# GpSimd's low parts of the weights: one 1024-column instruction per unit in place of four of 256 columns

## The chip, the cores and the metric

The kernel runs on one core of a Trainium2 chip. A core has TensorE (PE in the profile), VectorE (DVE), ScalarE (ACT), GpSimd (POOL), and SyncE (SP), which here only issues transfers. They run side by side, each through its own list of instructions in order, and wait for one another with semaphores. Data lies in SBUF (128 partitions); products land in PSUM, whose tiles the profile calls `bank`. The metric is the device time of one execution in microseconds (us), lower being better; for the kernel before, the median of three runs.

## The reference

Two transformer blocks in float32, on x of 512 tokens by 1024 channels:

```python
def first_block(x, ...):
    h = rmsnorm(x, ln1[l])
    z = jnp.einsum('btd,de->bte', h, w_in[l])
    u_pool, gq, gk, gv, gg, ga, fq, fk, fv, ff = jnp.split(z, pts, axis=-1)
    y_pool = pool_mixer(u_pool, ...)       # trailing means over 2, 4, 8, 16 tokens
    y_gla = gla_mixer(gq, gk, gv, gg, ga, ...)   # gated linear attention, chunks of 64
    y_fox = fox_mixer(fq, fk, fv, ff, b_f[l])    # softmax attention with a forget term F
    x = x + jnp.einsum('btd,de->bte', concatenate([y_pool, y_gla, y_fox]), w_o[l])
    h = rmsnorm(x, ln2[l])
    gate, up = split(h @ w_gu[l])
    x = x + (silu(gate) * up) @ w_down[l]
    return rmsnorm(x, ln_f)

def second_block(x, ...):
    q_lat, c_kv, k_rope, z_a, q_b, k_b, v_b, z_b, q_idx, k_idx, w_idx, gate_a, gate_b = split(rmsnorm_2(x) @ w_in)
    y_a = mla_attention(...) * silu(z_a)   # 8 heads, keys and values out of a latent
    y_b = dsa_attention(...) * silu(z_b)   # top-128 keys of each query by an index score
    merged = sigmoid(gate_a) * (y_a @ w_o_a) + sigmoid(gate_b) * (y_b @ w_o_b)
    return rmsnorm_2(x + merged @ w_out)
```

All the weight matrices together are read once, as 162 pieces of 512 KB.

## The kernel before

Every float32 product is made of three products of rounded (fp32r) numbers: high part by high part, low by high, high by low (lines 1379, 1381 and 1383, or 1393 to 1395 and 1405 to 1407 where the weights are what moves or the width differs). So each weight is needed as a high and a low part.

**The stream of weights.** A unit is eight weight tiles of 128x128, a piece of 128x1024 float32. SP loads units in order into the three buffers of `WS` (line 1256). For unit u, ACT copies `WS` to `WH`, which rounds it (line 1565, 161 times); then DVE or GpSimd subtracts, `WL = WS - WH` (DVE at line 1816, GpSimd at line 2164); then PE may use the unit. `WH` and `WL` have four buffers. Which engine makes `WL` is decided when the unit's step is planned, by a Python variable: `now["low"]` is `w_low_v` (DVE) at first, `w_low_g` (GpSimd) from line 762, in the middle of the GLA stage, to the end of FoX and of `w_o` (line 811), DVE again for the feed-forward part, GpSimd from line 1047 through the attention of the second block, and DVE from line 1193. That makes 97 units for DVE and 64 for GpSimd.

GpSimd does a unit in four instructions of 256 columns. Each first waits for the GpSimd instruction before it (`before[0]`) and for the unit's high part. The first three report an intermediate name `(u, c)` for which no other engine waits; the last one reports u. For that report PE waits before the unit's first product, and SP before it loads unit u+3, since the `WS` buffer is read until then:

```python
def split_low(u):
    return unit_low[u](u)
...
    if n >= NST:                                   # SP, in load(); NST is 3
        q.wait_ge(split_low(n - NST))
    e.dma_start(WS[:, n % NST, :], wall[n])
```

**The order of the work.** A planner written in Python makes one list, `steps`; every engine's program goes through that list and picks its own instructions. Nothing is reordered later. So an instruction that waits holds up all that stands behind it on its engine.

GpSimd's other work: the trailing means (`p_a`, `p_d`, lines 2184 to 2197), the fills of the FoX stacks `f_s` and `f_m` (lines 2170 to 2176, four memsets for each of four stacks, the last four at about 133 us), sums of squares (`acc`, lines 2204 and 2207), the product of gate and up in the feed-forward part (`fa`, line 2212) and a merge (line 2216).

SP's other work matters at one place. A FoX stack takes its forget rows and a copy of its other half by transfers (`stack_rows`, lines 1288 and 1290, and `stack_high`, lines 1297 and 1301), and these stand in the same list of SP behind loads of units. PE's first logits of that pair (line 1480) wait for the transfer of `f_m`.

DVE's work beside its own low parts: the scaling of products, the forget sums (`fw`, the scan `F`, a cast to `part`, `F` less `part`; lines 1852 to 1860), the GLA state (`g_S`, line 1934), softmax sums and scales (lines 1963 to 1978), the norms, and in the second block the index scores (lines 2067 and 2070: `score = i_t * wi + score`) with the search of the top 128 (`MAX8`, `MATCH_REPLACE8`, lines 2079 and 2081). The planner weaves one step of the search between two scalings.

Of the kernel before, what the change touches and what calls it, by code (L numbers as in the profile page):

```python
# [25 lines left out]
NST, NW = 3, 4  # L26
# [122 lines left out]
def f32(ap):  # L149
    return ap.bitcast(F32)  # L150
# [13 lines left out]
def build(nc, wall, xT, vecs, wa, wp, relb, cf, cph, coh, cb, scratch, outT):  # L164
    plan = []
    ctx = ExitStack()
    with ctx:
# [6 lines left out]
        def fixed(name, shape, dt=F32):  # L174
            size = int(np.prod(shape[1:])) * (2 if dt == BF16 else 4)
            t = at(name, shape, dt, place["at"])
            place["at"] += (size + 31) // 32 * 32
            return t
# [4 lines left out]
        WS = fixed("WS", [128, NST, UT * 128])  # L183
        WH = fixed("WH", [128, NW, UT * 128], F32R)
        WL = fixed("WL", [128, NW, UT * 128], F32R)
# [121 lines left out]
        def signal(name, by=1):  # L307
            signals.append(Signal(ctx.enter_context(nc.semaphore(name)), by))
            return signals[-1]
# [13 lines left out]
        w_hi, w_low_v, w_low_g = signal("w_hi"), signal("w_low_v"), signal("w_low_g")  # L323
# [871 lines left out]
        for m in range(8):  # L1195
            g, q = gt_ring.take(), mt_ring.take()
# [940 lines left out]
        def gpsimd_program(q):  # L2137
            e = q.e
            before = [None]

            def tick(signal, *names):

                before[0] = signal(names[0])
                return signal.tick(*names)

            for kind, s in steps:
                if kind == "start":
                    q.wait_ge(before[0])
                    e.memset(ones[:, :], 1.0).then_inc(*tick(fill, "ones"))
                    q.wait_ge(before[0])  # L2150
                    e.memset(eps[:, :], EPS).then_inc(*tick(fill, "eps"))
                    q.wait_ge(before[0])
                    e.memset(g_S[:, :, :], 0.0).then_inc(*tick(fill, "g_S"))
                    q.wait_ge(before[0])
                    e.memset(g_at[:, :, :, :], 0.0).then_inc(*tick(fill, "g_at"))
                    q.wait_ge(before[0])
                    e.memset(fw3[fr, :], 1.0).then_inc(*tick(fill, "w3"))
                elif kind == "split":
                    u = s["u"]
                    if unit_low[u] is w_low_g:  # L2160
                        for c in range(4):
                            cs = slice(256 * c, 256 * c + 256)
                            q.wait_ge(before[0], w_hi(u))
                            e.tensor_tensor(WL[:, u % NW, cs], WS[:, u % NST, cs], f32(WH[:, u % NW, cs]),  # L2164
                                            ALU.subtract).then_inc(*tick(w_low_g, u if c == 3 else (u, c)))
                elif kind in ("stack_fill", "stack_fill_late"):
                    for i, hl in ((1, 1),) if kind == "stack_fill_late" else ((0, 0), (0, 1), (1, 0)):
                        o = 64 - 64 * hl
                        q.wait_ge(before[0], gla_p(("y", 1)) if (i, hl) == (1, 1) else pool_g("end"))
                        e.memset(f32(f_s2[i][hl][o:o + 64, :]), 0.0).then_inc(*tick(fill, ("zero q", i, hl)))  # L2170
                        q.wait_ge(before[0])
                        e.memset(f32(f_m2[i][hl][o:o + 64, :]), 0.0).then_inc(*tick(fill, ("zero k", i, hl)))
                        q.wait_ge(before[0])
                        e.memset(f32(f_s2[i][hl][o:o + 6, :]), -1.0).then_inc(*tick(fill, ("minus", i, hl)))
                        q.wait_ge(before[0])
                        e.memset(f32(f_m2[i][hl][o:o + 6, :]), 1.0).then_inc(*tick(fill, ("stack", i, hl)))
                elif kind == "pool_means":
                    for n, b in enumerate((p_u, *p_a)):
                        q.wait_ge(before[0])
                        e.memset(b[:, :, 0:16], 0.0).then_inc(*tick(pool_g, ("zero", n)))  # L2180
                    src, w = p_u, 1
                    span = slice(16, 16 + T)
                    for step in range(4):
                        dst = p_a[step % 2]
                        own = slice(step // 2, 2)
                        q.wait_ge(before[0], out_v("pu1"), gla_v(("bc", 1)),
                                  pool_g(("sub", step - 1)) if step else pool_g(("zero", 2)))
                        e.tensor_tensor(dst[:, own, span], src[:, own, span], src[:, own, 16 - w:16 - w + T],
                                        ALU.add).then_inc(*tick(pool_g, ("sum", step)))
                        w *= 2  # L2190
                        j, r = step // 2, slice(64 * (step % 2), 64 * (step % 2) + 64)
                        q.wait_ge(before[0], pool_g(("sum", step)), consts_in())
                        e.tensor_tensor(p_d[r, j, :], dst[r, j, span], icnt[r, j, :], ALU.mult).then_inc(
                            *tick(pool_g, ("mean", step)))
                        q.wait_ge(before[0], pool_g(("mean", step)))
                        e.tensor_tensor(p_d[r, j, :], p_d[r, j, :], p_u[r, j, span], ALU.subtract).then_inc(
                            *tick(pool_g, ("sub", step), *(["end"] if step == 3 else [])))
                        src = dst
                elif kind == "square" and s["line"] is total_g:
                    what, m = s["key"]  # L2200
                    a = acc[1] if what in ("n3f", "lk") else acc[0]
                    q.wait_ge(before[0], square(s["key"]))
                    if m == 0:
                        e.tensor_copy(a[:, :], s["s"][:, :]).then_inc(*tick(total_g, s["key"]))
                    else:
                        q.wait_ge(before[0], total_g((what, m - 1)))
                        e.tensor_tensor(a[:, :], a[:, :], s["s"][:, :], ALU.add).then_inc(*tick(total_g, s["key"]))
                elif kind == "ffn_up":
                    jj = s["jj"]
                    a = fa[jj % 3]  # L2210
                    q.wait_ge(before[0], out_v(("up", jj)))
                    e.tensor_tensor(a[:, :], a[:, :], fg[jj % 3][:, :], ALU.mult).then_inc(*tick(gate_up, jj))  # L2212
                elif kind == "merge":
                    m, h = s["m"], s["q"]
                    q.wait_ge(before[0], out_v(("ogb", m)))
                    e.tensor_tensor(h[:, :], a_half[m][:, :], h[:, :], ALU.add).then_inc(*tick(merge, m))


        for program in (sync_program, tensor_program, scalar_program, vector_program, gpsimd_program):
            program(Queue(Counting(), counting=True))  # L2220
# [17 lines left out]
        @block.gpsimd  # L2238
        def _(eng):
            gpsimd_program(Queue(eng))  # L2240
# [114 lines left out]
```

## Time and profile before

| | |
|---|---|
| median of 3 runs | 1088.99 us (1088.71 to 1089.34) |
| the profiled execution | 1088.71 us, its span 1086.9 us |
| mean granted clock of TensorE | 0.988 of full speed |
| PE busy | 1049.1 us, 97% of the span |
| DVE busy | 583.4 us, 54% |
| ACT busy | 461.4 us, 42% |
| POOL busy | 299.1 us, 28%, 347 instructions |
| the chain that ended last, by engine | PE 80%, DVE 10%, ACT 5%, issue 3%, POOL 1%, DMA 1% |

All times inside the profile count from the start of the span. The 1.8 us between the span and the execution's own time lie around it. "PEclk" in a row on a window is the granted clock: 1.00 is 2.4 GHz and 0.50 is 1.2 GHz. "xN" is a count of instructions, and a row with xN above 1 in a timeline covers instructions in a row with their gaps. An arrow in a wait names what ended it.

### The profile page before, as it was taken

To read this page: it belongs to the slowest core of one execution; us is meant where nothing else is said; L and a number is where in the kernel's file an instruction comes from. 1 tells how busy PE (TensorE), PEld (TensorE's weight loads), DVE (VectorE), ACT (ScalarE), POOL (GpSimd) and SP (SyncE) were. 2 spreads that over 40 slices of the span, in tenths; PEclk is the share of its full clock that TensorE was granted. 3 is DMA by queue.
4 is the path that set the end of the run, shared out by engine and by line. 5 is a ranking of instruction groups with operands and counts; after the bars stand their busy time and mean duration, and the time that the engine had idled before them with its cause. 6 is when DMAs were issued, how large, how long until landed. Compare 5 with 4: busy or idle time off the path is not lost.

```text
span 1086.9 us, 13673 instructions
## 1 busy us (share of the span) xinstructions
PE 1049.1 (97%) x5152; PEld 846.4 (78%) x5160; DVE 583.4 (54%) x1049; ACT 461.4 (42%) x808; POOL 299.1 (28%) x347
## 2 busy tenths in 40 slices
PE   7998989999999999999999999799999999999996
PEld 6877787767888888888888777577787777788885
DVE  6584355647444433344444545798745655325544
ACT  6325436646222221222233556645764554423322
POOL 1373253323101000010113425533424334431100
PEclk9998899999999999999999999999999999999998
DMA  7211142212332332223232225312222333222312
GB/s 284 72 59 60 34 122 81 80 58 78 97 107 87 107 125 78 84 91 104 90 116 95 93 82 188 105 56 68 71 86 78 100 114 107 73 96 85 111 64 78
DMA packets 34801, 102.33 MB, mean 94 GB/s; under 512 B 4560, under 2 KB 8032, under 8 KB 34736
## 3 DMA queue, kind: packets, MB, share of 16 engines
q1 hardware_dynamic: 34736, 101.47, 28.6%
q8 instruction: 41, 0.67, 0.3%
q14 instruction: 24, 0.20, 0.1%
HBM read 93.35 MB, written 4.74 MB: 90 GB/s over the span
## 4 chain that ended last, share of the span: by engine, by line
PE 80%; DVE 10%; ACT 5%; issue 3%; POOL 1%; DMA 1%; SPq 0%; DVEq 0%; ACTq 0%; POOLq 0%
PE bank L1379 22%; PE bank L1381 21%; PE bank L1383 21%; PE bank L1513 3%; PE bank L1504 2%; PE bank L1393 2%; PE bank L1394 2%; PE bank L1395 2%; DVE m L2079 1%; DVE score L2081 1%; PE bank L1485 1%; DVE g_S L1934 1%; DVE score L2070 1%; PE bank L1460 1%; ACT WH L1565 1%
## 5 line engine op out<-in xcount | busy, mean ns | idle before, releaser
L1379 PE MATMUL bank<-HH,WH 128*128 128x512 f32 x808 | 328.2, 406 | 7.2 <-ACT HH L1573 6.1
L1383 PE MATMUL bank<-HH,WL 128*128 128x512 f32 x808 | 317.2, 393 | 0.0
L1381 PE MATMUL bank<-HL,WH 128*128 128x512 f32 x808 | 317.0, 392 | 0.0
L2164 POOL TENSOR_TENSOR WL<-WS,WH 128x256 fp32r<-128x256 f32 x256 | 201.9, 789 | 316.3 <-ACT WH L1565 300.6
L1379 PEld LDWEIGHTS bank<-HH,WH 128*128 128x128 f32 x808 | 153.7, 190 | 42.6 <-ACT WH L1569 6.1
L1565 ACT ACTIVATE WH<-WS 128x1024 fp32r<-128x1024 f32 x161 | 167.5, 1047 | 41.3 <-PE bank L1383 41.0
L1383 PEld LDWEIGHTS bank<-HH,WL 128*128 128x128 f32 x808 | 152.8, 189 | 33.0
L1381 PEld LDWEIGHTS bank<-HL,WH 128*128 128x128 f32 x808 | 153.3, 190 | 29.3 <-issue 0.5
L1816 DVE TENSOR_TENSOR WL<-WS,WH 128x1024 fp32r<-128x1024 f32 x97 | 126.4, 1309 | 34.1 <-ACT WH L1565 34.1
L2212 POOL TENSOR_TENSOR fa<-fa,fg 128x512 f32<-128x512 f32 x22 | 28.3, 1286 | 271.6 <-DVE fa L2016 271.6
L1379 PE MATMUL bank<-GH,WH 128*128 128x512 f32 x176 | 68.5, 389 | 0.0
L1381 PE MATMUL bank<-GL,WH 128*128 128x512 f32 x176 | 68.5, 389 | 0.0
L1383 PE MATMUL bank<-GH,WL 128*128 128x512 f32 x176 | 68.5, 389 | 0.0
L1996 DVE TENSOR_TENSOR X<-X,bank 128x512 f32<-128x512 f32 x39 | 26.7, 685 | 71.1 <-PE bank L1383 70.8
L1712 ACT ACTIVATE GH<-fa 128x512 fp32r<-128x512 f32 x22 | 13.9, 632 | 114.6 <-POOL fa L2212 114.6
L1393 PE MATMUL bank<-WH,HH 128*128 128x256 f32 x160 | 49.4, 309 | 2.3 <-ACT f_v L1595 1.2
L1577 ACT ACTIVATE sq<-X 128x512 f32<-128x512 f32 x31 | 19.5, 629 | 73.3 <-DVE X L1996 73.2
L1680 ACT ACTIVATE PT<-bank 128x128 f32<-128x128 f32 (+1 forms) x96 | 41.2, 429 | 18.8 <-PE bank L1504 18.5
L1394 PE MATMUL bank<-WL,HH 128*128 128x256 f32 x160 | 46.8, 292 | 0.0
L1395 PE MATMUL bank<-WH,HL 128*128 128x256 f32 x160 | 46.7, 292 | 0.0
L1963 DVE TENSOR_REDUCE small<-bank 128x1 f32<-128x128 f32 (+1 forms) x64 | 30.8, 482 | 19.4 <-PE bank L1486 12.4
L2018 DVE TENSOR_TENSOR GL<-fa,GH 128x512 fp32r<-128x512 f32 x22 | 15.2, 693 | 47.1 <-ACT GH L1712 47.1
(335 smaller groups left out, 1685.1 us busy)
## 6 DMA issues: line engine op xcount, KB each, us to landing
WS<-wall SPq DMA_DIRECT2D x161, 512.0 KB, 3.4
scratch<-rows SPq DMA_DIRECT2D x8, 320.0 KB, 4.7
X<-xT SPq DMA_DIRECT2D x8, 256.0 KB, 6.8
b_t<-scratch SPq DMA_DIRECT2D x8, 256.0 KB, 3.6
outT<-X SPq DMA_DIRECT2D x8, 256.0 KB, 2.1
b_m<-b_m SPq DMA_DIRECT2D x11, 128.0 KB, 2.3
f_s<-f_s SPq DMA_DIRECT2D x8, 128.0 KB
f_m<-f_m SPq DMA_DIRECT2D x8, 128.0 KB
```

The costliest lines, as they stand in the source:

```text
L1379: e.matmul(b[:, :], wh, xh[:, at_k, :], start=k == 0, stop=False)
L1381: e.matmul(b[:, :], wh, xl[:, at_k, :], start=False, stop=False)
L1383: m = e.matmul(b[:, :], wl, xh[:, at_k, :], start=False, stop=k == n - 1)
L1393: e.matmul(b[:, 0:256], xh[:, k, cs], wh, start=k == 0, stop=False)
L1394: e.matmul(b[:, 0:256], xh[:, k, cs], wl, start=False, stop=False)
L1395: m = e.matmul(b[:, 0:256], xl[:, k, cs], wh, start=False, stop=k == NK - 1)
L1513: m = e.matmul(b[64 * hl:64 * hl + 64, 128 * kb:512], v[:, kb, hd * 64:hd * 64 + 64], s["pt"][:, at_pt + 128 * kb:at_pt + 512], start=kb = ...
L1565: e.activation(WH[:, u % NW, :], WS[:, u % NST, :], ACT.Copy).then_inc(*w_hi.tick(u))
L1680: e.activation(dst, s["b"][:, 0:128 * i + 128].rearrange("p (a n) -> p a n", n=128), ACT.Copy).then_inc(*moved.tick(s["u"]))
L1816: e.tensor_tensor(WL[:, u % NW, :], WS[:, u % NST, :], f32(WH[:, u % NW, :]), ALU.subtract).then_inc(*w_low_v.tick(u))
L1963: e.tensor_reduce(st[:, 0:1], s["b"][:, 0:n], AX, ALU.max, negate=True).then_inc(*neg_max.tick(u))
L2164: e.tensor_tensor(WL[:, u % NW, cs], WS[:, u % NST, cs], f32(WH[:, u % NW, cs]), ALU.subtract).then_inc(*tick(w_low_g, u if c == 3 else (u ...
```

## The change

The loop over four column chunks is gone. One `tensor_tensor` subtracts all 1024 columns of the unit, after one wait for the GpSimd instruction before it and for the unit's high part, and it reports u once. 256 instructions become 64. The data, the buffers, the units that go to GpSimd, and the order of all steps on every engine stay as they are.

```diff
--- before.py
+++ after.py
@@ -2158,11 +2158,9 @@
                 elif kind == "split":
                     u = s["u"]
                     if unit_low[u] is w_low_g:
-                        for c in range(4):
-                            cs = slice(256 * c, 256 * c + 256)
-                            q.wait_ge(before[0], w_hi(u))
-                            e.tensor_tensor(WL[:, u % NW, cs], WS[:, u % NST, cs], f32(WH[:, u % NW, cs]),
-                                            ALU.subtract).then_inc(*tick(w_low_g, u if c == 3 else (u, c)))
+                        q.wait_ge(before[0], w_hi(u))
+                        e.tensor_tensor(WL[:, u % NW, :], WS[:, u % NST, :], f32(WH[:, u % NW, :]),
+                                        ALU.subtract).then_inc(*tick(w_low_g, u))
                 elif kind in ("stack_fill", "stack_fill_late"):
                     for i, hl in ((1, 1),) if kind == "stack_fill_late" else ((0, 0), (0, 1), (1, 0)):
                         o = 64 - 64 * hl
```

## Rows read from the trace of the kernel before

**Rows 1.** The page, busy time in us (share of the span) x instructions.
```profile
PE 1049.1 (97%) x5152; PEld 846.4 (78%) x5160; DVE 583.4 (54%) x1049; ACT 461.4 (42%) x808; POOL 299.1 (28%) x347
```

**Rows 2.** Waits of PE: waited for, us in total, times, longest.
```profile
PE bank L1455 <- DVE g_S L1934: 4.9, 2, 2.5
PE bank L1480 <- DMA f_m<-f_m: 2.8, 1, 2.8
PE bank L1405 <- DVE zb L1838: 2.8, 1, 2.8
PE bank L1412 <- POOL acc L2207: 2.5, 1, 2.5
...
PE bank L1393 <- ACT f_v L1595: 1.2, 1, 1.2
```

**Rows 3.** Groups of POOL by form: xcount | busy us, mean ns | idle before.
```profile
L2164 POOL TENSOR_TENSOR WL<-WS,WH 128x256 fp32r<-128x256 f32 x256 | 201.9, 789 | 316.3 <-ACT WH L1565 300.6
L2212 POOL TENSOR_TENSOR fa<-fa,fg 128x512 f32<-128x512 f32 x22 | 28.3, 1286 | 271.6 <-DVE fa L2016 271.6
...
L2188 POOL TENSOR_TENSOR p_a<-p_a 128x1024 f32<-128x1024 f32 x1 | 1.9, 1892 | 0.1
```

**Rows 4.** One source line, L2164: duration ns min/median/max, first and last start.
```profile
L2164 POOL TENSOR_TENSOR WL<-WS,WH x256: 722/738/1531, 72.1 to 964.3; 128x256 fp32r<-128x256 f32 x128
```

**Rows 5.** Timeline of POOL: start us, us, instruction xcount [idle before].
```profile
72.06 4.37 POOL L2164 TENSOR_TENSOR WL<-WS,WH 128x256 fp32r<-128x256 f32 x4
...
130.32 3.19 POOL L2164 TENSOR_TENSOR WL<-WS,WH 128x256 fp32r<-128x256 f32 x4 [15.39 <-ACT WH L1565]
...
135.90 7.44 POOL L2164 TENSOR_TENSOR WL<-WS,WH 128x256 fp32r<-128x256 f32 x8
...
668.23 4.17 POOL L2164 TENSOR_TENSOR WL<-WS,WH 128x256 fp32r<-128x256 f32 x4 [5.73 <-ACT WH L1565]
...
675.26 3.71 POOL L2164 TENSOR_TENSOR WL<-WS,WH 128x256 fp32r<-128x256 f32 x4 [0.75 <-ACT WH L1565]
```

**Rows 6.** Timeline of DVE, same columns.
```profile
42.65 1.22 DVE L1882 TENSOR_TENSOR_SCAN g_b<-rset,sq 128x512 f32<-128x512 f32 x1
...
72.25 1.10 DVE L1852 TENSOR_TENSOR fw<-fw,fw 8x512 f32<-8x512 f32 x1
...
77.01 0.42 DVE L1857 CAST part<-F 8x512 fp32r<-8x512 f32 x1
77.47 0.68 DVE L1860 TENSOR_TENSOR F<-F,part 8x512 f32<-8x512 f32 x1
...
99.45 1.08 DVE L1946 TENSOR_TENSOR g_q<-g_q,tmp 128x512 f32<-128x512 f32 x1 [6.27 <-ACT tmp L1651]
...
668.60 3.20 DVE L2070 SCALAR_TENSOR_TENSOR score<-i_t,wi,score 128x512 f32<-128x512 f32 x3 [4.78 <-ACT i_t L1763]
...
674.98 0.74 DVE L2070 SCALAR_TENSOR_TENSOR score<-i_t,wi,score 128x512 f32<-128x512 f32 x1
...
675.83 0.71 DVE L2067 TENSOR_SCALAR score<-i_t,wi 128x384 f32<-128x384 f32 x1
...
679.39 0.68 DVE L2090 TENSOR_TENSOR tmp<-bank,Rb 128x512 f32<-128x512 f32 x1
...
697.83 0.95 DVE L2070 SCALAR_TENSOR_TENSOR score<-i_t,wi,score 128x256 f32<-128x256 f32 x1
...
702.99 0.65 DVE L2070 SCALAR_TENSOR_TENSOR score<-i_t,wi,score 128x256 f32<-128x256 f32 x1
```

**Rows 7.** Chain of waits that ends at PE's start at 145.75.
```profile
139.44 0.33 SPq L1256
...
143.31 2.31 DMA f_m<-f_m
```

**Rows 8.** Windows: busy us (xcount) per engine, PEclk, DMA share, GB/s.
```profile
145.40:148.80 3.40, 3.05 (x15) 3.08 (x16) 0.74 (x3) 1.90 (x4) 0.35 (x1) 0.50 0.74 221
679.00:684.00 5.00, 2.46 (x9) 1.43 (x9) 3.59 (x5) 3.88 (x7) 2.38 (x3) 1.00 0.74 240
```

## The prediction

> **What bounds the kernel now.** I read the busy shares first: PE is busy for 97% of the span and POOL for 28% [rows 1], so the change can pay only through PE's few waits. The list of those waits comes next. No wait in it is for a low part from POOL. It waits 4.9 us in two pieces for the GLA state `g_S`, 2.8 us for the FoX stack `f_m`, 2.8 us for `zb`, 2.5 us for `acc` and 1.2 us for `f_v` [rows 2]. Then I read POOL's prices [rows 3, 4], and last the timelines of POOL and DVE around each of those waits [rows 5, 6], the chain behind `f_m` [rows 7] and the granted clock in two windows [rows 8]. Two things in them matter: where a unit ends earlier on POOL than before, and what DVE does while POOL is in one.
>
> **What an instruction of 1024 columns costs.** The trace has no such subtraction. Units now take 3.19 us where DVE leaves POOL alone (the one at 130.32) [rows 5]: four times 0.738 [rows 4] and three gaps of 0.08. From 256 to 512 columns the time goes from 0.738 to 1.286 [rows 3, 4], 0.548 for 256 columns; two more such steps for each 512 give 0.738 + 3 x 0.548 = 2.38 us. The low end is the one row of 1024 columns, an addition in place: 1.89 us [rows 3]. The high end is four times 0.738, 2.95 us. I take 2.38, as the step comes from the nearest kinds of row: a unit then takes 0.8 us less alone, and 64 units 51 us less of an engine that isn't the bound.
>
> The Trainium skill ("GPSIMD Engine Reference", section 3.1) gives 4497 ns for a float32 tensor_tensor of 2048 columns; half of that is an estimate of 2.25 us, and the sum below would come out about 1 us lower by it.
>
> **What the change does to DVE.** A DVE operation that reads two operands from SBUF and starts within a POOL subtraction ends 0.55 us after POOL's instruction: the subtraction of `fw` started at 72.25 and ended at 73.35, the first chunk ended at 72.06 + 0.74 = 72.80; `g_q` at 99.45 ended at 100.53, POOL's last chunk at 99.99 [rows 5, 6]. A scaling in SBUF ends 0.2 us after it (675.83), a 256-column score 0.3 us (697.83). Operations that read PSUM aren't touched (679.39, 0.68). So far the wait is at most about one chunk; from now it is up to 2.4 us, but only once a unit instead of up to four times.
>
> The Trainium skill ("SBUF — State Buffer", section "Who interferes with whom") says the same against this change: the two engines share a pair of ports as an exclusive lock held for the whole instruction, and the loser blocks. The trace agrees, with the 0.55 us above. By a reading of that rule with DVE in front of every unit, rival C below follows.
>
> **The sum, place by place** (at 2.38 us; ends for 1.89 and 2.95 in brackets).
>
> 1. GLA state, 72 us. The unit ends at 74.44 in place of 76.43. `fw` ends at 74.44 + 0.55 = 74.99; then a scan of 1.22, a cast of 0.42 and a subtraction of 0.68, now alone [rows 6]: 77.31. Before, the cast after it started at 77.01. Add 0.05 of gaps: **+0.4**, which PE's first wait for `g_S` passes on [0; +1.0].
> 2. `g_q`, 99.45. Two units of 6.44 us from 93.55 end by 98.4 at the latest, before it starts. It takes 0.68 instead of 1.08, and PE's wait for `f_v` shrinks: **-0.4** [-0.4; 0].
> 3. FoX stack, 130 to 146. The chain is: unit at 130.32, four memsets, unit at 135.90, whose end at 139.42 lets SP go on at 139.44 [rows 5, 7], then six transfers in SP's queue, the last issued at 143.31 and landed 2.31 us later [rows 7]. First unit 3.19 to 2.38, -0.81; memsets 135.90 - 133.51 = 2.39 as before; second unit from 3.52 to 2.38, -1.14. SP goes on 1.95 us earlier, all of it on the path of `f_m`, and PE's wait goes from 2.8 to 0.9: **-1.95** [-2.8, the whole wait; -0.8].
> 4. The clock behind it. In the 3.4 us after that wait PE was granted 0.50 [rows 8], and did what takes 1.7 us at full clock. After the wait of 2.5 us for `acc` the clock stayed at 1.00 [rows 8], so a wait alone doesn't bring the fall; with two thirds of it gone I expect none: **-1.7** [-1.7; 0].
> 5. Short of slack in three more places: a softmax scaling on DVE at 190.6, the squares loop at 246 to 262, the softmax beside the unit at 870. The same rule delays DVE by 1 to 2 us in each, and PE's share of it, after its slack there, I estimate at 0.4, 0.4 and 0.8: **+1.6** [0; +2.5].
> 6. The index scores, 668 to 705, where PE waits for DVE. The unit at 668.23 now holds three scores, 3.20 us in all [rows 6]. After: POOL ends at 670.61, the first score at 671.16, two more at 0.74: 672.64 instead of 671.80, **+0.85**. The second unit (675.26) starts that much later, and 0.3 behind the score at 674.98; POOL ends at 678.8, the scaling of 675.83 at 679.0 instead of 676.54, +2.45, of which the next score gives 0.3 back. So `tmp` (679.39), on which PE's wait for `acc` hangs, is **+2.15 to +2.4** late. The unit at 682.81 adds 0.4 before `zb`; the scores at 697.83 and 702.99 end 0.3 us behind a whole unit instead of a chunk, +0.85 and +0.6. DVE has no idle time between them to give it back: **+4.2** together [+2.0; +6.5].
>
> Everything else of the 64 units I price at nothing. The cover is PE's distance to these units: its list of waits names POOL for `acc` alone [rows 2]. If that cover went, SP's loads would be late, but they too only get earlier with a shorter unit. The 192 waits and signals that go were waited for by nobody.
>
> Sum: 0.4 - 0.4 - 1.95 - 1.7 + 1.6 + 4.2 = +2.15 us. The profiled execution took 1088.71 (its span and 1.8 around it), so 1090.9; that execution is 0.3 below the median of 1088.99. About 0.2% (2.2 us) is what a measurement here can tell from no change.
>
> **The rivals.**
>
> A, faster. POOL's wide instruction costs what the `p_a` row says, 1.89 us. For: it is the only row of this width. Against: it reads one tile twice, not two tiles, and writes no fp32r. Then 0 - 0.4 - 2.8 - 1.7 + 0.3 + 2.0 = -2.6: 1086.1. It decides below about 2.15 us an instruction.
>
> B, no change. DVE's waits are absorbed: the scores have room that I don't see, since the planner puts search steps between scalings, and term 6 comes to 2 while the clock still falls at 145.4. 0.4 - 0.4 - 1.95 + 0.8 + 2.0 = +0.9, about 1089.6. For: the PE waits in rows 2 are few, and DVE is busy for 54% alone [rows 1]. Against: its idle time isn't at 668 to 705.
>
> C, clearly slower. DVE is caught by more whole units in 668 to 705, and PE's wait for `acc` grows from 2.5 to 4.9 us; the granted clock, 1.00 there now [rows 8], falls behind it as it does at 145.4. At half clock for 3.4 us that costs 1.7 more, and with term 3 at its small end (-1.1) the sum is 2.15 + 1.7 + 0.85 = +4.7: 1093.4. At 2.95 us an instruction it would be +1.0 - 0.8 + 2.5 + 6.5 - 0.4 - 0.9 = +7.9, 1096.6. For: one 1.0 window after a 2.5 us wait says nothing of 4.9. Against: PE has just had a long dense stretch.
>
> **How the numbers follow.** My forecast 0.48, A 0.17, B 0.18, C 0.17. The forecast spreads 2 us to both sides (its own range 1088.7 to 1093.0), so half of it lies above 1091.2 (0.24), 0.22 within 0.2% and 0.02 below. B is within 0.2% with 0.16 and below with 0.02; A is faster with 0.13 and within with 0.04; C is slower. Slower: 0.24 + 0.17 = 0.41; same 0.22 + 0.16 + 0.04 = 0.42; faster 0.17. The range runs from A's 1086.1 to 1095.0, inside C's worse end.
>
> **What would show it.** POOL's group of `WL` x64 with a mean near 2.4 us (term by term: 1.9 is A). SP's L1256 at 137.5 on the old time, PE's wait for `f_m` at 0.9, PEclk 1.00 behind it. DVE's `fw` at 2.7 us, and scaling L2067 at 675 us near 3 us. PE's waits for `acc` and `a_q` up by 2 and 1 us. The prediction is wrong if the wait for `f_m` stays (something else than POOL held SP), or if DVE's excess in 668 to 705 doesn't move PE.

## The result, and the profile after

The changed kernel takes 1094.38 us in the median of 4 runs (1093.08 to 1095.98), the kernel before beside it 1088.85 (1086.74 to 1089.34). The ratio is 1.0052, with a 95% interval of 1.0040 to 1.0065: it is slower by 4.4 to 7.1 us, clear of noise. The forecast was 1090.9 in a range of 1086.1 to 1095.0. The range held it, by 0.6 us, but the likeliest case fell short by 3.5 us, and of a difference of 5.5 us it had 2.

The busy shares of the changed kernel, and its groups and the source line of the new instruction:

```profile
PE 1052.5 (96%) x5152; PEld 846.5 (77%) x5160; DVE 609.8 (56%) x1049; ACT 460.0 (42%) x808; POOL 252.1 (23%) x155
...
L2162 POOL TENSOR_TENSOR WL<-WS,WH 128x1024 fp32r<-128x1024 f32 x64 | 155.0, 2421 | 358.0 <-ACT WH L1565 357.4
...
L2162 POOL TENSOR_TENSOR WL<-WS,WH x64: 2347/2397/2734, 71.5 to 967.7; 128x1024 fp32r<-128x1024 f32 x64
```

Against [rows 1, 3, 4]: POOL loses 47 us of work and DVE gains 26 (583.4 to 609.8), with the same instructions on DVE: that is time in which DVE waits for POOL inside its operations, as the single ones below show. The new instruction has a median of 2.397 us; 2.38 was forecast.

PE's waits (waited for: us in total, times, longest), for comparison with [rows 2]:

```profile
PE bank L1455 <- DVE g_S L1934: 5.2, 2, 3.0
PE bank L1412 <- POOL acc L2205: 4.4, 1, 4.4
PE bank L1379 <- DVE a_q L2106: 3.1, 2, 1.9
...
PE bank L1405 <- DVE zb L1838: 1.6, 1, 1.6
PE bank L1513 <- ACT PT L1680: 1.6, 3, 0.8
...
PE bank L1480 <- DMA f_m<-f_m: 1.0, 1, 1.0
...
PE bank L1531 <- ACT i_t L1763: 0.9, 1, 0.9
```

The wait for `f_m` went from 2.8 to 1.0 us, that for `acc` from 2.5 to 4.4, that for `a_q` from 1.6 to 3.1, and that for `zb` fell from 2.8 to 1.6. The other changes and new waits are of 0.9 us or less each.

DVE and POOL at the places of [rows 5, 6] (start, duration, instruction):

```profile
71.68 2.74 DVE L1852 TENSOR_TENSOR fw<-fw,fw 8x512 f32<-8x512 f32 x1
...
666.95 4.29 DVE L2070 SCALAR_TENSOR_TENSOR score<-i_t,wi,score 128x512 f32<-128x512 f32 x3 [5.37 <-ACT i_t L1763]
...
675.24 2.37 DVE L2067 TENSOR_SCALAR score<-i_t,wi 128x384 f32<-128x384 f32 x1
...
680.16 0.69 DVE L2090 TENSOR_TENSOR tmp<-bank,Rb 128x512 f32<-128x512 f32 x1
...
699.02 1.79 DVE L2070 SCALAR_TENSOR_TENSOR score<-i_t,wi,score 128x256 f32<-128x256 f32 x1
...
705.02 1.22 DVE L2070 SCALAR_TENSOR_TENSOR score<-i_t,wi,score 128x256 f32<-128x256 f32 x1
...
876.23 2.41 DVE L2039 TENSOR_TENSOR b_s<-b_st,b_s 64x512 fp32r<-64x512 f32 x1 [1.68 <-ACT b_s L1745]
...
886.94 1.97 DVE L1978 TENSOR_SCALAR Pc<-Pc,small 128x128 f32<-128x128 f32 x1
...
71.48 2.40 POOL L2162 TENSOR_TENSOR WL<-WS,WH 128x1024 fp32r<-128x1024 f32 x1
...
129.72 2.41 POOL L2162 TENSOR_TENSOR WL<-WS,WH 128x1024 fp32r<-128x1024 f32 x1 [16.11 <-ACT WH L1565]
...
134.53 4.88 POOL L2162 TENSOR_TENSOR WL<-WS,WH 128x1024 fp32r<-128x1024 f32 x2
...
666.58 2.41 POOL L2162 TENSOR_TENSOR WL<-WS,WH 128x1024 fp32r<-128x1024 f32 x1 [6.32 <-ACT WH L1565]
...
674.70 2.69 POOL L2162 TENSOR_TENSOR WL<-WS,WH 128x1024 fp32r<-128x1024 f32 x1 [0.78 <-ACT WH L1565]
...
875.69 2.41 POOL L2162 TENSOR_TENSOR WL<-WS,WH 128x1024 fp32r<-128x1024 f32 x1 [5.22 <-ACT WH L1565]
886.42 2.40 POOL L2162 TENSOR_TENSOR WL<-WS,WH 128x1024 fp32r<-128x1024 f32 x1 [8.32 <-ACT WH L1565]
```

The subtraction of `fw` takes 2.74 us (1.10 before), the three scores 4.29 (3.20), the scaling at 675 us 2.37 (0.71). The lengthened operations start while POOL is in its instruction (`fw` 0.2 us after POOL's start, the scaling and `b_s` 0.54) and end 0.1 to 0.6 us behind POOL's end.

The granted clock (windows: busy us of PE, PEld, DVE, ACT, POOL, then PEclk, DMA share, GB/s):

```profile
145.40:148.80 3.40, 3.40 (x30) 3.36 (x30) 1.70 (x3) 3.38 (x8) 3.04 (x2) 1.00 0.08 26
683.80:687.90 4.10, 4.10 (x15) 3.14 (x14) 3.96 (x5) 4.04 (x6) 2.42 (x1) 0.60 0.16 28
707.20:711.00 3.80, 3.80 (x13) 3.01 (x12) 2.83 (x6) 0.00 (x0) 0.00 (x0) 0.55 0.31 114
```

The window that stood at 0.50 before is at 1.00 [rows 8], and there are two new stretches at half clock of 3.4 us each, the first behind the longer wait for `acc`, the second behind that for `a_q`. (The windows are a little wider than the stretches, hence 0.60 and 0.55.)

**Where the time went.** PE's instructions are the same in both traces, so each can be matched with its partner, and the lag of the changed kernel read along the program. The two profiled executions took 1088.71 and 1095.55 us. The lag, in us, grows or shrinks by:

| place (us in the kernel before) | forecast | in the traces |
|---|---|---|
| before the first wide unit | 0 | -0.5 (chance: no difference in the programs) |
| 72 to 103, terms 1 and 2 | 0 | 0.0 |
| 130 to 149, terms 3 and 4 | -3.65 | -3.1 (wait -1.9, clock -1.4, of which 0.1 comes back by 166) |
| 190 and 246 to 263, of term 5 | +0.8 | +1.4 |
| 668 to 705, term 6 | +4.2 | +4.8 (waits for `i_t` and `acc` 3.0, half clock behind `acc` 1.6, `zb` -1.2, `a_q` 1.4) |
| half clock behind `a_q`, at 707 | 0 | +1.6 |
| 870 to 884, of term 5 | +0.8 | +2.5 |
| sum | +2.15 | +6.7 |

The medians differ by 5.5 us and not by 6.7: of the changed kernel's 15 single executions (1092.8 to 1096.0 us) only one was slower than the profiled one. The first row and what is said of the clock below are reasons not to read any row to better than half a microsecond.

### The profile page after: what moved, and what is told of

The parts are those of the page before. It is cut to its first block, busy times and chain, and to the rows that moved or that the text cites. A ratio compares the mean times of both kernels' runs of the same rounds, so it can differ in the third digit from the quotient of the medians.

```text
span 1093.8 us, 13481 instructions
## 1 busy us (share of the span) xinstructions
PE 1052.5 (96%) x5152; PEld 846.5 (77%) x5160; DVE 609.8 (56%) x1049; ACT 460.0 (42%) x808; POOL 252.1 (23%) x155
## 4 chain that ended last, share of the span: by engine, by line
PE 75%; DVE 12%; ACT 5%; issue 4%; SPq 2%; DMA 1%; POOL 1%; DVEq 0%; ACTq 0%; POOLq 0%
PE bank L1379 20%; PE bank L1383 20%; PE bank L1381 20%; PE bank L1513 3%; PE bank L1504 2%; PE bank L1393 2%; PE bank L1394 2%; PE bank L1395 2%; DVE m L2079 1%; DVE score L2070 1%; DVE score L2081 1%; PE bank L1485 1%; DVE acc L1835 1%; DVE g_S L1934 1%; ACT WH L1565 1%
## 5 line engine op out<-in xcount | busy, mean ns | idle before, releaser
L2162 POOL TENSOR_TENSOR WL<-WS,WH 128x1024 fp32r<-128x1024 f32 x64 | 155.0, 2421 | 358.0 <-ACT WH L1565 357.4
L1708 ACT ACTIVATE fs<-fg 128x512 f32<-128x512 f32 x22 | 13.9, 632 | 59.6 <-DVE fg L2007 59.6
```

What stands on the lines that cost most here:

```text
L2162: e.tensor_tensor(WL[:, u % NW, :], WS[:, u % NST, :], f32(WH[:, u % NW, :]), ALU.subtract).then_inc(*tick(w_low_g, u))
```

## Experiments

All are timed in five rounds beside the kernel before on the same chip. On the later chips that kernel had medians of 1089.75 to 1092.11 us and single executions from 1086.7 to 1094.0, so the ratio of a run tells more than its absolute time. In its 69 single executions there the mean granted clock ran from 0.982 to 0.989, and the time with it: the 20 at 0.983 or less took 1092.2 us in the mean, the 10 at 0.988 or more 1088.5. The profiled execution (1088.71 us, 0.988) is among the fastest, and every lag below is counted against it. All but the two runs of "Who starts first" differ from the kernel before in how many instructions make a unit (the last of the n reports u, which isn't shown here):

```diff
-                        for c in range(4):
-                            cs = slice(256 * c, 256 * c + 256)
+                        n = 1 if u < 34 else 4      # each run has its own rule here
+                        w = UT * 128 // n
+                        for c in range(n):
+                            cs = slice(w * c, w * c + w)
```

### One block at a time

Rule of the first: `1 if u < 34 else 4`. Rule of the second: `4 if u < 34 else 1`.

> One instruction of 1024 columns only for units 12 to 33 (GLA, FoX, w_o), four of 256 for units 103 to 144. Theory (each place by itself, the harm is DVE's wait in the second block): the gains at the FoX stack (wait for f_m 2.8 to 1.0, full clock behind it, together -3.5) less the delays at 72, 190 and 246 to 263 (+1.5): 1.7 to 2.2 us faster than before, 1086.7 to 1087.2. Rival (wide instructions cost time wherever DVE works): no faster than before, 1088.5 or more.

> One instruction only for units 103 to 144 (second block), four for units 12 to 33. Theory: DVE's waits move PE by 4.3 at the scores, two falls of the granted clock cost 3.2 less 1.1 given back at zb, and the softmax at 870 to 895 gives 2.5: 7.5 to 9 us slower than before, 1096.5 to 1098. Rival (the loss comes with the earlier arrival of the second block after the first block's gain, other overlaps of loads and products): no more than 5.5 us, the loss of the whole change, 1094.5 at most.

Measured: the first block alone 1087.73 us, ratio 0.9971 (0.9957 to 0.9984), 3.2 us faster; the second block alone 1100.65 us, ratio 1.0086 (1.0065 to 1.0106), 9.4 us slower. The two add up to 6.2 where the whole change has 5.7. So it is two changes of opposite sign in one edit, and the rival of a general loss falls, as does that of a loss which needs the first block's gain. Both kernels have the places of the whole: in the profile of the second, the lag behind the kernel before grows by 1.2 and 1.9 at the waits for `i_t` and `acc`, by 0.85 and 1.8 at those for `a_q`, and by 2.5 between 870 and 884. Two more things stand in these profiles. That of the second block has half clock from 103.0 to 109.8 us, where its program is still that of the kernel before, which has full clock there; this costs it 2.9 us by chance. And in that of the first block, whose units beside the scores are the old ones, PE arrives at 660 with a lead of 2.7 us and keeps 1.65: it waits 3.6 us for `acc`, in place of 2.5. A lead isn't kept in full where PE waits for DVE next.

### Two units, and the right two units

> One instruction only for units 17 and 18, those in front of the FoX stack's transfers. Theory: the whole gain of the change is here: the end of unit 18 on SP 1.95 us earlier, the wait for f_m 0.9 to 1.0, and PEclk 1.00 behind it: 3.3 to 3.7 us faster, 1085.3 to 1085.7. Rival (the clock falls anyway, or the gain needs unit 16 and 19 too): 2 us or less, 1087 or more.

The rule is `1 if u in (17, 18) else 4`. Measured: 1088.62 us, ratio 0.9979 (0.9966 to 0.9992), 2.3 us faster (2.0 by the medians), and the wait for `f_m` at 1.7 us. That is near the rival, which had said that unit 16 was needed too, and far from the theory. The reason is in its trace:

```profile
133.01 3.19 POOL L2166 TENSOR_TENSOR WL<-WS,WH 128x256 fp32r<-128x256 f32 x4 [15.38 <-ACT WH L1565]
...
138.59 5.20 POOL L2166 TENSOR_TENSOR WL<-WS,WH 128x1024 fp32r<-128x1024 f32 x2
...
PE bank L1480 <- DMA f_m<-f_m: 1.7, 1, 1.7
...
PE bank L1480 <- DMA f_m<-f_m: 0.9, 1, 0.9
```

The unit before the memsets still has four instructions; the first unit of the stream is made in two halves, and I had counted those as two units. The wide ones were the unit at 135.9 and the next. What I had priced for the unit at 135.9 alone is 1.1 of the 1.95 us, and 2.8 - 1.1 = 1.7 is what is found. The last row above is of the corrected run, `1 if u in (16, 17) else 4`:

> One instruction of 1024 columns only for units 16 and 17, the two around the memsets at 130.3 and 135.9. (The earlier run with two units had numbers one too high: it took the units at 135.9 and 139.5.) Theory: f_m's wait 0.9 to 1.0 instead of 2.8, from 0.8 of the first unit and 1.1 of the second, and no clock fall behind it: the kernel otherwise as before, 2 to 3.5 us faster, near the version that leaves out the harmful units. Rival (the gain needs other wide units of the stage too): f_m's wait 1.7 as with one unit, 1 to 2 us faster.

Measured: 1085.88 us, ratio 0.9957 (0.9943 to 0.9971), 4.7 us faster, wait 0.9 us. Two wide units hold the whole gain of the change. The 4.7 aren't all wait: in the trace PE gains 3.3 us here (1.9 of wait, 1.4 of clock) and loses 1.2 again to half clock behind `zb` (687.5 to 691.0), and its single executions were granted 0.988 to 0.991, those of the kernel before beside them 0.982 to 0.989.

### Six units beside the scores

> One instruction only for units 106 to 111, beside the index scores. Theory: these six of 64 carry most of the loss: a_q 4.2 us later, clock falls behind the waits for acc and a_q (3.2 in all), 1.1 given back at zb: 5.5 to 6.5 us slower, 1094.5 to 1095.5. Rival (the clock fell in the whole change for another reason, such as what PE did before): 4 to 4.5 us and PEclk 1.00 at 683 to 711.

Here too the numbers were one too high: these are the units from 675.3 to 711.5, without the one at 668.2. Measured: 1095.43 us, ratio 1.0046 (1.0030 to 1.0062), 5.0 us slower, and the granted clock half at 680.2 to 687.1 and 707.5 to 711.0. The time lies between the two numbers and can't tell them apart; the clock does, and the rival with a full clock is out.

### Half as long

Rule: `2`, everywhere.

> Two instructions of 512 columns per unit, everywhere. Theory (what DVE loses goes with the length of the one instruction that it meets): a unit alone 2 x 1.29 + 0.08 = 2.65 us; subtraction of fw near 1.6 us (1.10 before, 2.74 with 1024 columns); the unit in front of SP's transfers gives 1.3 us of the 1.95; a third to a half of DVE's loss at the scores: 0 to 3 us slower than before in all. Rival (DVE's loss goes with POOL's total time in units, which falls): faster than before by about 1.5 us.

Measured: 1088.77 us, ratio 0.9984 (0.9975 to 0.9993): 1.7 us faster, the rival's number. Its trace:

```profile
L2166 POOL TENSOR_TENSOR WL<-WS,WH 128x512 fp32r<-128x512 f32 x128 | 171.5, 1340 | 338.3 <-ACT WH L1565 332.6
...
71.17 1.64 DVE L1852 TENSOR_TENSOR fw<-fw,fw 8x512 f32<-8x512 f32 x1
...
666.38 4.03 DVE L2070 SCALAR_TENSOR_TENSOR score<-i_t,wi,score 128x512 f32<-128x512 f32 x3 [5.32 <-ACT i_t L1763]
...
674.40 1.26 DVE L2067 TENSOR_SCALAR score<-i_t,wi 128x384 f32<-128x384 f32 x1
...
PE bank L1480 <- DMA f_m<-f_m: 1.5, 1, 1.5
PE bank L1379 <- DVE a_q L2106: 1.3, 1, 1.3
```

The single operations grow with the length of the instruction that they meet, as the theory has it, though POOL's total time falls: `fw` 1.64 us between 1.10 and 2.74, the scores 4.03 between 3.20 and 4.29, the scaling 1.26 between 0.71 and 2.37. So the rival's reason isn't borne out by them. The scores have three quarters of the full loss already, where I had expected a third to a half. What I had wrong above all is the sum. In this trace PE gains 1.3 us at `f_m` and 1.4 of clock behind it, and loses 2.5 at `i_t` and `acc`, half clock included; but the waits for `a_q` and in the softmax, which cost the changed kernel 5.5 us with the half clock, don't grow at all. The loss at such a place begins only where the slack ends, and the gain at `f_m` has no slack in front of it.

### Who starts first

The changed kernel, in which POOL's unit 130 also waits for DVE's `b_s`:

```diff
-                        q.wait_ge(before[0], w_hi(u))
+                        q.wait_ge(before[0], w_hi(u), bstack_v(("q", 5)) if u == 130 else None)
```

> The changed kernel, in which POOL also waits, before unit 130 (the one at 875.7), for DVE's subtraction b_s that started 0.5 us after it and took 2.41. Only the order of the two starts changes. Theory (the pair of ports is held for the whole instruction, by who starts first): b_s back at 0.7 us, the unit a microsecond late without harm, PE 0.9 to 1.3 us earlier from there on. Rival (b_s is slow for another reason, or PE waits there for the unit): b_s or PE no faster, PE's lag over the kernel before unchanged at 2.2 us between 870 and 900.

Measured: 1095.50 us, ratio 1.0043 (1.0026 to 1.0059), as the change itself. POOL and DVE of this run:

```profile
876.68 2.39 POOL L2162 TENSOR_TENSOR WL<-WS,WH 128x1024 fp32r<-128x1024 f32 x1 [6.63 <-DVE b_s L2039]
...
875.82 0.69 DVE L2039 TENSOR_TENSOR b_s<-b_st,b_s 64x512 fp32r<-64x512 f32 x1 [1.68 <-ACT b_s L1745]
...
876.74 2.48 DVE L1978 TENSOR_SCALAR Pc<-Pc,small 128x256 f32<-128x256 f32 x1
...
886.93 1.97 DVE L1978 TENSOR_SCALAR Pc<-Pc,small 128x128 f32<-128x128 f32 x1
```

`b_s` is back at 0.69 us, from 2.41: which of the two starts first decides who waits. But PE gains nothing. POOL now starts at 876.68 (875.69 in the changed kernel), and the softmax scaling of 876.74, 0.53 us before the change, takes 2.48. The wait moved to the next operation. So I let the two units wait for the scalings as well, after which DVE has a stretch of PSUM work:

```diff
+                        room = {130: share_v(("dsa", 3, 1)), 131: share_v(("dsa", 4, 0))}
+                        q.wait_ge(before[0], w_hi(u), room.get(u))
```

> The changed kernel, in which POOL's units 130 and 131 also wait for the softmax scalings of DVE that they would meet (L1978 at 876.7 and 886.9); behind those DVE reads PSUM for 2.4 us. Theory (what is hit is whatever two-operand or scaling work starts within the instruction; a start in a stretch without such work costs nothing): b_s 0.7, both scalings 0.3 to 0.5, and PE's lag of 2.2 to 2.8 us between 870 and 900 gone: 2.2 to 2.8 us faster than the run in which only b_s was spared (1095.5), 1092.7 to 1093.3. Rival (the wait moves on again to the next operation, or PE then waits for the units): under 1 us faster.

Measured: 1092.15 us, ratio 1.0014 (1.0004 to 1.0025), 3.3 us below the run before by median and 0.3% by ratio. PE's lag grows by 0.3 us between 870 and 900 instead of 2.5. Part of the rest of the 3.3 is the clock, which in this profile didn't fall behind `a_q`. The wait moved on here too: the next scaling, at 884.94, takes 1.33 us where the same one of the kernel before takes 0.35, but it is short enough for PE's slack. DVE of this run:

```profile
873.97 0.69 DVE L2039 TENSOR_TENSOR b_s<-b_st,b_s 64x512 fp32r<-64x512 f32 x1 [1.68 <-ACT b_s L1745]
...
874.88 0.35 DVE L1978 TENSOR_SCALAR Pc<-Pc,small 128x256 f32<-128x256 f32 x1
...
883.25 0.29 DVE L1978 TENSOR_SCALAR Pc<-Pc,small 128x128 f32<-128x128 f32 x1
```

### Only where it pays, and shorter where it hurts

Rules: `1 if 12 <= u <= 23 or 25 <= u <= 29 else 4`, then the same with 8 for units 105 to 110, then with 8 for every other unit; and one run with wide units only from 111 on.

> One instruction of 1024 columns for units 12 to 23 and 25 to 29 of the first block, four of 256 for the units at 72, 190, 246, 252 and 258 us and for the second block. Theory: the whole gain at the FoX stack (f_m wait 1.0) and none of the delays at 72, 190 and 246 to 263: 1.5 us faster than one instruction in all of the first block and 4 to 5 us faster than the kernel before. Rival (those delays are hidden, or come with the other units): the same as all of the first block, 3 us faster than before.

> One instruction only for units 111 to 144, behind the scores; four for all before. Theory (the softmax between 870 and 900 is the only place there): 2.2 to 2.7 us slower than before, no fall of the granted clock beyond those of the kernel before. Rival (most of this came with the lateness of the scores): under 1 us.

> The version with one instruction for units 12 to 23 and 25 to 29, and eight instructions of 128 columns for units 105 to 110 beside the index scores (four for the rest). Theory (DVE's wait goes with the length of the one instruction): each hit costs 0.3 us less than with 256 columns, PE's waits for acc and a_q shrink by 0.5 to 1 in all: 0.5 to 1 us faster than with four there (1085.8). Rival (each end of a chunk is another chance to lose the ports, so more and shorter hits): the same or slower, and POOL's unit over 4.5 us.

> One instruction of 1024 columns where it pays (units 12 to 23 and 25 to 29), eight of 128 columns for every other unit of POOL (at 72, 190, 246 to 262 us and the whole second block), not only for the six beside the scores. Theory (short where DVE works beside): the forget sum at 72, the squares loop at 246 to 262 and the softmax gain 0.2 to 0.6 each: 0.5 to 1.5 us faster than with eight beside the scores alone (1082.7), 1081.2 to 1082.2. Rival (those places have slack, or POOL's longer units of 4.2 us make PE or SP late): the same or slower than 1082.7.

| kernel | median us | ratio to before (95%) |
|---|---|---|
| e7: wide where it pays, else 4 | 1085.77 | 0.9954 (0.9939 to 0.9970) |
| e8: wide from unit 111 on, else 4 | 1092.34 | 1.0015 (1.0000 to 1.0030) |
| e11: as e7, 8 beside the scores | 1082.67 | 0.9929 (0.9915 to 0.9944) |
| e12: as e7, 8 in place of every 4 | 1082.64 | 0.9915 (0.9901 to 0.9928) |

e7 lies where theory had it, 5 us faster by ratio (4.4 by median), and can't be told from the two-unit run. e8 is 2.2 us slower by median and 1.6 by ratio, with an interval that touches no change and single executions from 1089.4 to 1096.4 (granted clock 0.990 to 0.981); in its trace, which is that of the fastest one, the lag grows by 2.5 us at the same softmax operations (`b_s` 2.40 us, scaling 1.97), and nowhere else for good. The six units beside the scores and the 34 from 111 on (unit 111 is in both) cost 6.6 us together, the whole second block 9.4; what the other units hold of the rest can't be told within these intervals. e11 gained 3.1 us more than e7 by median and 2.7 by ratio, not the 0.5 to 1 of the theory. Its POOL, DVE and waits:

```profile
L2166 POOL TENSOR_TENSOR WL<-WS,WH 128x128 fp32r<-128x128 f32 x48 | 25.9, 541 | 13.9 <-ACT WH L1565 10.4
...
664.02 5.85 POOL L2166 TENSOR_TENSOR WL<-WS,WH 128x128 fp32r<-128x128 f32 x8 [6.11 <-ACT WH L1565]
...
664.39 2.49 DVE L2070 SCALAR_TENSOR_TENSOR score<-i_t,wi,score 128x512 f32<-128x512 f32 x3 [5.16 <-ACT i_t L1763]
...
697.75 0.53 DVE L2070 SCALAR_TENSOR_TENSOR score<-i_t,wi,score 128x256 f32<-128x256 f32 x1
...
PE bank L1412 <- POOL acc L2209: 3.2, 1, 3.2
...
PE bank L1379 <- DVE a_q L2106: 1.2, 1, 1.2
```

The three scores take 2.49 us, in place of 3.20 with four instructions and 4.29 with one. POOL pays for it: its unit takes 5.85 us (4.17 and 2.41), and nobody waits for it. PE waits for `zb` 0.4 us instead of 2.8, and for `a_q` 1.2 us instead of 1.6. Not all of the 2.7 is DVE's. From 660 to 706 PE loses 1.4 us on the kernel before in e7's trace and gains 0.7 in e11's; 1.0 of that difference is a fall of the clock, which in e7 comes behind the wait for `zb` (687.4 to 690.8) and in e11 in front of it (679.3 to 682.7), where a shorter wait for `zb` makes up for it. Each length of instruction is thus a choice of who waits for whom. e12 has the same time as e11; its ratio is lower, but the intervals overlap. In its trace PE has one new wait of 1.5 us for a low part, near 86 us, behind a unit that took POOL 6.20 us at 70.7: the rival's point. Both beat the kernel before (by 0.7 to 0.85%) and the changed one.

## Why the prediction was right in part

**The price of the instruction, and term 3: right.** 2.397 us against 2.38. SP goes on at the end of the second unit, which is 134.53 + 4.88/2 = 136.97 in the changed kernel and 139.42 in the one before; the six transfers and their 2.3 us come behind as before, and PE's wait is 1.0 us (0.9 forecast). The run with two wide units shows that nothing else is needed for this.

**Terms 1 and 2: right.** The wait for `g_S` grew by 0.3 us in all and that for `f_v` shrank by 0.4.

**Term 4, the clock behind `f_m`: the sign right, its size not.** The same work took 1.2 to 1.4 us less, not 1.7: the stretch at half clock began at 145.40, inside the wait, and PE was busy for only 3.05 of its 3.40 us [rows 8]. And the fall isn't certain. Of the profiles in which PE waited 2.8 us or more for `f_m`, two have it (this kernel before, and the second block alone, where it lasts 7 us) and two don't (the six units, and wide from 111 on). Of the ten with a wait of 1.7 us or less none has it. So as an expectation the term should have been about half as large.

**Term 6 on DVE: right to 0.1 us, in part by luck.** `tmp` at 679.39 comes 0.8 us later while the stage starts 1.65 earlier: +2.4 (2.15 to 2.4 forecast). `a_q` (703.56) comes 2.60 later, +4.25 (4.2 forecast). But the sentence that DVE has no idle time between them is wrong. The two scores at 682.62 take 1.63 us longer (1.62 to 3.25), and an idle time of 1.25 us in front of line 2099 takes up most of it. The scaling at 691.84, which the sum doesn't have, takes 1.45 us longer (0.35 to 1.80), and idle times in front of the next scores take up all of it.

**What term 6 left out in front of the stage.** PE comes to it 2.24 us earlier than before, and DVE only 1.65. The 0.6 us between them are a load. The copy to `WH` that stands in ACT's list before `i_t` waits for its `WS`, which it didn't before (the second row is of the kernel before):

```profile
665.38 1.06 ACT L1565 ACTIVATE WH<-WS 128x1024 fp32r<-128x1024 f32 x1 [0.57 <-DMA WS<-wall]
...
667.02 1.06 ACT L1565 ACTIVATE WH<-WS 128x1024 fp32r<-128x1024 f32 x1
```

So +4.25 on DVE is +4.8 on PE. The prediction had said that loads only get earlier; they do (SP issues this one 1.7 us earlier), but by less than PE does.

**The step that failed on the clock** is that the sum has no term for it in the second block. I had put the fall behind `acc` into rival C, with 0.17 in all, because the row of the kernel before showed 1.00 there [rows 8]. That one row was the exception: in all 13 profiles of the other kernels here a fall begins between 678 and 688 us, also in those whose wait for `acc` is 2.5 to 2.9 us. So that fall isn't shown to be an effect of the change. Behind `a_q` it falls in four of the five in which the two waits come to 3.0 us or more (the changed kernel, the second block alone, the six units, and the one with only `b_s` spared), and in none of the nine profiles with 1.7 us or less. Rival C had a fall behind a longer wait, at 1.7 us and at the wrong place: what was lost behind `acc` (1.6 us) was largely repaid at `zb`, where PE would have waited anyway; what was lost behind `a_q` (1.6 us) was not, since PE doesn't wait for DVE again soon there.

**Term 5, the softmax at 870: mis-sized.** It was priced as one delay of 1 to 2 us beside one unit, of which 0.8 would reach PE; no row stood behind that share. It measured +2.5, because two units are involved: `b_s` waits for the first (0.74 to 2.41), and a scaling at 886.9 waits for the second (0.30 to 1.97), where before it met the end of one chunk and lost nothing. In the kernel before:

```profile
871.21 0.74 DVE L2039 TENSOR_TENSOR b_s<-b_st,b_s 64x512 fp32r<-64x512 f32 x1 [1.68 <-ACT b_s L1745]
...
880.41 0.30 DVE L1978 TENSOR_SCALAR Pc<-Pc,small 128x128 f32<-128x128 f32 x1
```

The first costs PE 1.6 us, the second 0.9. By then the slack was used up. The two other places of term 5 were priced at 0.8 and measured 1.4. Of rival B nothing is left; the run that let the units start behind those operations got 2.2 of the 2.5 us back.

**The account.** Of the 5 us by which the rows of the table behind its first pass the forecast, 2.3 are term 5, 1.6 the clock behind `a_q`, 0.6 the load in front of term 6 and 0.5 term 4. The mechanism was right, the terms for the softmax and for the clock were too small, and the range reached to 1095.0 only because rival C had been priced.

The rule of the Trainium skill ("SBUF — State Buffer", section "Who interferes with whom") on the lock bore the DVE side throughout. Its remark that issue order decides who blocks is what the runs with moved starts show, 2.41 to 0.69 us for the same operation. By a long lock alone, halves should have made the kernel slower than quarters. The scores are slower (3.20 to 4.03 us), the kernel isn't: it gains at `f_m`, and behind the scores DVE's delays fall into slack.

**Left open.** Why the clock falls after one wait and not after another of the same length; how much of the 5.5 us is the clock. The 15 single executions of the changed kernel were granted 0.984 to 0.987, which lies within the 0.982 to 0.989 of the kernel before on the later chips; the profile of the kernel before, with 0.988, is one of its lucky ones.

## What to carry to other kernels

An instruction's width on GpSimd is a choice of who waits: wide ones finish a unit sooner and hold DVE's two-operand work and its scalings in SBUF for their whole length; narrow ones cost GpSimd time and set DVE free. Use width by place: wide where someone waits for GpSimd's result, narrow where DVE is behind and nobody waits for GpSimd. And a granted clock read in one profile is one draw: compare it with the clocks of several executions before a term rests on it.

## What the runs showed of the hardware

POOL's subtraction took 0.453 us at the least for 128 columns, 0.738 us in the median for 256 and 2.397 us for 1024 (for 512 the mean was 1.340 us). The step of 0.548 us for 256 columns, taken from another operation, held up to 1024 (2.38 forecast); the one row of that width in the trace before, an addition of 1.89 us, didn't carry over, and with that rival A fell.

DVE's reductions to the top eight, and its operations that read PSUM, kept their duration beside POOL in every run (0.68 to 0.70 us for 512 columns), so the same POOL instruction is free in one half microsecond and costs 2 us in the next. A start moved by 1 us (875.69 to 876.68) moved a wait of 1.7 us from `b_s` to a scaling (0.53 to 2.48).
